# Up projections of a split-fp32 decoder trunk: six products of 288 columns a weight tile, against five of 384, 384, 384, 384 and 192

## What is computed

```python
h = rmsnorm(x, p["ffn_norm"][layer])
up = h @ p["w_up"][layer]                    # D_MODEL 1024 -> 2 * D_FF = 5632
c, fb = causal_dwconv(up, ffn_bufs[layer], p["ffn_conv_w"][layer], p["ffn_conv_b"][layer])   # 3 taps
x = x + (jax.nn.silu(c[..., :D_FF]) * c[..., D_FF:]) @ p["w_down"][layer]
```

## Time and profile before

| | |
|---|---|
| median of 3 runs | 1236.5 us (1236.37 to 1237.01) |
| the profiled execution's own time | 1235.46 us |
| its span | 1233.7 us |
| TensorE busy with matmuls | 1210.8 us (98%), 8828 matmuls |
| VectorE, ScalarE, GpSimd busy | 672.0, 455.9, 550.9 us (54%, 37%, 45%) |
| chain that ended last | 93% TensorE |

### The profile page before, as it was taken

One profiled execution on the slowest core, in us unless ns is written; L12 is line 12 of the kernel. 1 busy time (PEld: TensorE's weight loads), 2 busy tenths in 40 slices (PEclk: granted clock), 3 DMA queues, 4 the chain that ended last, 5 costly groups with the idle time before them and its releaser, 6 DMA issues.

```text
span 1233.7 us, 22991 instructions
## 1 busy us (share of the span) xinstructions
PE 1210.8 (98%) x8828; PEld 1180.7 (96%) x8828; DVE 672.0 (54%) x1080; ACT 455.9 (37%) x677; POOL 550.9 (45%) x524
## 2 busy tenths in 40 slices
PE   7999999999999999999999999999999999999996
PEld 7887899999999999999999999999999999999996
DVE  5999466786136741365513754377821676216742
ACT  7333364433123331234512533344321434214354
POOL 4643345565345443453455224346543454435430
PEclk9999999999999999999999999999999999999998
DMA  6310133222312223222422222222322222222222
GB/s 236 110 44 18 44 97 101 71 88 82 103 69 85 85 69 103 69 81 65 156 77 85 79 68 69 86 69 76 94 86 86 69 85 85 86 86 69 85 65 78
DMA packets 33636, 103.57 MB, mean 84 GB/s; under 512 B 4880, under 2 KB 6928, under 8 KB 33552
## 3 DMA queue, kind: packets, MB, share of 16 engines
q1 hardware_dynamic: 29344, 98.40, 24.5%
q10 hardware_dynamic: 4224, 4.22, 1.1%
HBM read 98.29 MB, written 4.79 MB: 84 GB/s over the span
## 4 chain that ended last, share of the span: by engine, by line
PE 93%; DVE 2%; ACT 2%; POOL 1%; issue 1%; DMA 0%; ACTq 0%; SPq 0%; DVEq 0%
PE psum L315 87%; PE psum L409 3%; DVE squares_sum L1466 1%; PE psum L353 1%; PE psum L560 1%; POOL w_lo L995 0%; DVE residual L1163 0%; PE psum L361 0%; ACT arena L917 0%; DVE arena L1435 0%; DMA w_raw<-in_w_in_ab 0%; PE psum L429 0%; DVE arena L1458 0%; ACT w_hi L625 0%; PE psum L423 0%
## 5 line engine op out<-in xcount | busy, mean ns | idle before, releaser
L995 POOL TENSOR_TENSOR w_lo<-w_raw,w_hi 128x1024 fp32r<-128x1024 f32 (+2 forms) x188 | 437.0, 2327 | 504.0 <-ACT w_hi L625 504.0
L315 PE MATMUL psum<-x_hi,w_hi 128*128 128x288 f32 x1856 | 401.7, 298 | 6.4 <-ACT w_hi L625 6.4
L315 PE MATMUL psum<-x_hi,w_lo 128*128 128x288 f32 x1856 | 398.0, 296 | 1.1 <-POOL w_lo L995 1.1
L315 PE MATMUL psum<-x_lo,w_hi 128*128 128x288 f32 x1856 | 397.8, 296 | 0.0
L315 PEld LDWEIGHTS psum<-x_hi,w_hi 128*128 128x128 f32 x1856 | 299.6, 189 | 8.6 <-ACT w_hi L625 6.4
L315 PEld LDWEIGHTS psum<-x_hi,w_lo 128*128 128x128 f32 x1856 | 299.6, 189 | 1.5 <-POOL w_lo L995 1.5
L315 PEld LDWEIGHTS psum<-x_lo,w_hi 128*128 128x128 f32 x1856 | 299.8, 189 | 0.0
L625 ACT ACTIVATE w_hi<-w_raw 128x1024 fp32r<-128x1024 f32 (+2 forms) x188 | 187.1, 997 | 237.7 <-PE psum L315 222.5
L1397 DVE SCALAR_TENSOR_TENSOR arena<-arena,params 128x592 f32<-128x592 f32 x176 | 205.7, 1169 | 84.7 <-ACT arena L841 71.3
L315 PE MATMUL psum<-h_hi,w_hi 128*128 128x288 f32 x960 | 207.3, 297 | 3.7 <-DVE residual L1163 1.9
L315 PE MATMUL psum<-h_hi,w_lo 128*128 128x288 f32 x960 | 205.6, 296 | 0.0
(11 more groups left out here) (140 smaller groups left out, 693.8 us busy)
## 6 DMA issues: line engine op xcount, KB each, us to landing
w_raw<-in_w_up SPq DMA_DIRECT2D x88, 512.0 KB, 3.2
w_raw<-in_w_down SPq DMA_DIRECT2D x32, 512.0 KB, 3.5
w_raw<-in_w_in_c SPq DMA_DIRECT2D x16, 512.0 KB, 3.2
w_raw<-in_w_in_ab SPq DMA_DIRECT2D x12, 512.0 KB, 3.6
w_raw<-in_w_down SPq DMA_DIRECT2D x16, 384.0 KB, 3.2
w_raw<-in_w_out_ab SPq DMA_DIRECT2D x16, 256.0 KB, 2.6
w_raw<-in_w_out_c SPq DMA_DIRECT2D x8, 512.0 KB, 3.2
residual<-in_x SPq DMA_DIRECT2D x8, 288.0 KB, 6.3
```

The costliest lines, as they stand in the source:

```text
L315: last = nc.tensor.matmul(PS[:, 2 * (q % 2 if slot is None else slot) + half, 0:HALF], w[q][:, k * P:(k + 1) * P], r[:, r_at, half * HALF: ...
L995: nc.gpsimd.tensor_tensor(w_lo[slot][:, 0:nk * P], w_raw[slot % 2][:, 0:nk * P], w_hi[slot][:, 0:nk * P].bitcast(F32), ALU.subtract).then_ ...
```

## The change

The operands `xh` and `xl` become two planes of one tile `xs`, so that one access pattern can take the same tokens of both. In the up-projection units alone (`wide=True`) the 576 tokens are divided into 384 (`FRONT`) and 192 (`BACK`). Per input tile there are five matmuls: hi·hi, hi·lo and lo·hi over the front, lo·hi over the back, and one of 384 columns that takes the back of `xh` and of `xl` side by side against `w_hi`, so that hi·hi and hi·lo of the back land beside each other in one bank. The sum of those two is made when the unit is read out: ScalarE copies the hi·lo part from the accumulator to `mixed[:, j]`, VectorE adds it to the hi·hi part in place, and then scales as before in pieces of 384, 128 and 64.

```diff
+    FRONT = 2 * T // 3
+    BACK = T - FRONT
...
-        xh = sb("x_hi", [P, KD, T], F32R)
-        xl = sb("x_lo", [P, KD, T], F32R)
+        xs = sb("x_split", [P, KD, 2, T], F32R)
+        xh, xl = xs[:, :, 0, :], xs[:, :, 1, :]
...
+        mixed = cut(F1 + 2 * T + RT * D, 2, BACK)
...
+            def wide_products(q, k, first, final):
+
+                slot, cols = q % 2, slice(k * P, (k + 1) * P)
+                front, both = PS[:, 2 * slot, 0:FRONT], PS[:, 2 * slot + 1, 0:2 * BACK]
+                nc.tensor.matmul(front, w_hi[q][:, cols], xs[:, k, 0, 0:FRONT], start=first, stop=False)
+                nc.tensor.matmul(front, w_hi[q][:, cols], xs[:, k, 1, 0:FRONT], start=False, stop=False)
+                nc.tensor.matmul(both.rearrange("p (a t) -> p a t", a=2), w_hi[q][:, cols], xs[:, k, :, FRONT:T],
+                                 start=first, stop=False)
+                nc.tensor.matmul(front, w_lo[q][:, cols], xs[:, k, 0, 0:FRONT], start=False, stop=final)
+                return nc.tensor.matmul(PS[:, 2 * slot + 1, 0:BACK], w_lo[q][:, cols], xs[:, k, 0, FRONT:T],
+                                        start=False, stop=final)
...
+                    if wide:
+                        last = wide_products(q, k, at == 0, at == nk - 1)
+                    else:
+                        last = products(q, k, r0 + k, nk, rh, rl, at == 0, at == nk - 1)
...
+                            act.wait_ge(unit_done, i * 2 + (u0 + j + 1))
+                            nc.scalar.activation(mixed[:, j, :], PS[:, 2 * j + 1, BACK:2 * BACK], ACT.Copy)\
+                                .then_inc(mix_ready, 1)
                             if j == 0 and before is not None:
                                 product_hi(before)
...
+            def scaled_mixed(slot, u, dst, pad, at):
+
+                bank = PS[:, 2 * slot + 1, 0:BACK]
+                dve.wait_ge(mix_ready, at)
+                nc.vector.tensor_tensor(bank, bank, mixed[:, slot, :], ALU.add).then_inc(mix_added, 1)
+                nc.vector.tensor_tensor(dst[:, pad:pad + FRONT], PS[:, 2 * slot, 0:FRONT], rstd[:, 0:FRONT], ALU.mult)
+                dve.wait_ge(mix_added, at)
+                nc.vector.tensor_tensor(dst[:, pad + FRONT:pad + PR], bank[:, 0:PR - FRONT], rstd[:, FRONT:PR], ALU.mult)
+                n = NS * (pad + DS)
+                nc.vector.tensor_tensor(smp(dst[:, pad + PR:pad + PR + n], pad + DS)[:, :, pad:],
+                                        smp(bank[:, PR - FRONT:BACK]), smp(rstd[:, PR:T]), ALU.mult)\
+                    .then_inc(acc_free, 1)
...
-                            scaled_padded(j, u, up[:, j, :], FB)
+                            scaled_mixed(j, u, up[:, j, :], FB, (i + c0) * 2 + (j + 1))
```

More of the change, by code:

```diff
@@ L226, in hybrid_trunk @@
         st_out = sem("st_out")
+        mix_ready, mix_added = sem("mix_ready"), sem("mix_added")
         tap0_ready, tap1_ready, tap_ready = sem("tap0_ready"), sem("tap1_ready"), sem("tap_ready")
@@ L323, in weights, with unit @@
                     pe.wait_ge(acc_free, u - 1)
-            def unit(q, u, nk, rh, rl, ready=None, base=0, middle=None, r0=0, order=None):
+            def unit(q, u, nk, rh, rl, ready=None, base=0, middle=None, r0=0, order=None, wide=False):
                 weights(u)
@@ L331, in unit @@
                         pe.wait_ge(ready, base + at + 1)
-                    last = products(q, k, r0 + k, nk, rh, rl, at == 0, at == nk - 1)
+                    if wide:
+                        last = wide_products(q, k, at == 0, at == nk - 1)
+                    else:
+                        last = products(q, k, r0 + k, nk, rh, rl, at == 0, at == nk - 1)
                     if middle is not None and at == nk // 2:
@@ L480, in _, with plain_units @@
                 yb_unit(m)
-            def plain_units(u0, nk, rh, rl, n):
+            def plain_units(u0, nk, rh, rl, n, wide=False):
                 with pe.Fori(0, n // 4) as i:
                     for q in range(4):
-                        unit(q, i * 4 + (u0 + q), nk, rh, rl)
+                        unit(q, i * 4 + (u0 + q), nk, rh, rl, wide=wide)
             def ffn(layer):
@@ L494, in ffn @@
                     if g == 0:
-                        unit(0, u0, KD, xh, xl, xl_ready, KD * n)
+                        unit(0, u0, KD, xh, xl, xl_ready, KD * n, wide=True)
                         norm_sums(n, r)
@@ L501, in middle @@
                             spread(r)
[L502 to L505, removed]
+                        unit(1, u0 + 1, KD, xh, xl, middle=middle, wide=True)
+                        unit(2, u0 + 2, KD, xh, xl, wide=True)
+                        unit(3, u0 + 3, KD, xh, xl, wide=True)
+                        plain_units(u0 + 4, KD, xh, xl, 2 * nt - 4, wide=True)
                     else:
-                        plain_units(u0, KD, xh, xl, 2 * nt)
+                        plain_units(u0, KD, xh, xl, 2 * nt, wide=True)
                     ud = u0 + 2 * nt
```

## The result

The changed kernel takes 1246.68 us (median of 4 runs, 1245.86 to 1247.48) against 1236.43 before: 10.3 us slower, ratio 1.0083, 95% interval 1.0065 to 1.0100. The forecast was 1245, slower. The time came out as predicted, but two terms of the sum were wrong, by some 17 and 15 us in opposite directions, and the rows show it at once.

What follows compares the result with a forecast made beforehand. TensorE was taken as the bound, with the VectorE, ScalarE and GpSimd loop second and expected to take over. -12.0 (products) + 21.6 (waits) - 1.1 = +8.5 on 1235.5, so 1244, stated as 1245; range 1227 to 1262.

Steps and rivals of the forecast that it cites:

- What bounds: TensorE bounds at 12.80 us a pair of up tiles; the VectorE, ScalarE and GpSimd loop, 12.57, is second.
- TensorE's part: Up-unit matmuls: 162.5 ns per 384 columns, a 133 ns floor for 192; input tile 783 ns, -12.0 us in all.
- The loop's length: VectorE, ScalarE and GpSimd in group 0: five links of read-out, copy, taps and `w_lo` lengthen a pair from 12.57 to 13.3 us.
- The loop's waits: TensorE waiting on late read-outs in the up groups: 10.8 us a layer, +21.6 for both, less 1.1 already there.
- the cost at the short down projection: After group 2's 6 pairs the last product comes late for a short down projection: 2.5 us.
- the tile (783 ns): Sign: one input tile of an up unit, four products at 162.5 ns plus one at 133, would take 783 ns.
- the 13.3 us in group 2: Sign: read-outs would come every 13.3 us in groups 1 and 2 as in group 0.
- the 20 us of waits: Sign: TensorE's waits would name VectorE's last scaling, some 20 us in all, against next to none before.
- the free tap and the blocked one: Sign: on VectorE the first tap after j = 1 runs free; the second is blocked by GpSimd's `w_lo`, ending 0.63 later.
- The slow narrow product: Rival, chance 0.12: the 192-column product takes 323 ns, a tile 973 ns, +122 us, 1358.
- A fee on the wide product and the floor on the narrow one: Rival, 0.08 shared with a slow side-by-side operand: products 173 and 133 ns, tile 825, +21, 1257.
- The side-by-side operand: Rival, 0.08 shared with fee and floor: operand of two 192-column runs slower than a plain one; time between 1257 and 1358.

Runs made afterwards that it cites:

- x2: Kernel before the change, products of 288 kept, but read out with the change's copy and add (values wrong): 1243.51 us, ratio 1.0057.
- y4: The change with tokens divided 320 and 256 instead of 384 and 192, ScalarE's order unchanged, whole computation: 1245.70 us, ratio 1.0077.
- y2: The change with tokens divided 320 and 256, without copy and add at read-out (part of the sum left out): 1232.25 us, ratio 0.9968.
- x1: The change's five products (384 and 192), without copy and add at read-out (part of the sum left out): 1241.45 us, ratio 1.0040.
- y1: Kernel before the change with three products of 512 and three of 64 columns per input tile in up units, plain read-out: 1395.19 us, one execution.
- x3: The change with ScalarE's copy put ahead of the rounding of the weight tile: 1243.46 us, ratio 1.0056.
- x4: The change with ScalarE's copy for j = 1 put ahead of the silu of j = 0: 1242.85 us, ratio 1.0052.
- z1: The change (384 and 192) with the early copy of x4 and both roundings of a pair moved to its start: 1245.43 us, ratio 1.0078.
- z2: As z1, with tokens divided 320 and 256, whole computation: 1242.42 us, ratio 1.0052.

## Why the prediction was right, and where it was wrong

- **What bounds**: right. The loop of VectorE, ScalarE and GpSimd in groups 0 was a second bound within 0.23 us a pair of the first, and the change pushed it over. x2 shows its part alone.
- **TensorE's part: the wrong step.** The forecast took the 13 ns at 288 columns for a floor from the weight load, "and not like a fee on every matmul", from the plain fp32 type's 2 ns over. The fee is there at every width of fp32r tried, 13 ns at 256, 288 and 320, 14 at 384, 18 at 512. The real floor is the load's own turn, 0.111 us. The earlier trace rows showed it: (1.21 - 0.19) / 9 = 0.113 us, where the forecast divided 1.21 by 10 and then took 133 all the same. The products that go with those ten loads, of the plain fp32 type, have one column each and stand within 1.17 us, so narrow products that cost less than 133 ns were there to be seen:

```profile
23.36 1.17 PE L353 MATMUL psum<-ones,squares_sum 128*128 128x1 f32 x10
```

  So 162.5 should have been 174, and 133 should have been 111: 807 ns instead of 783, +4.9 us instead of -12.0. The forecast weighed a floor (783) against a fee (786) and found them nearly the same; there are both, and the larger of the two counts at each width. The upper bound of the 384 product, 173, was the truth within 1 ns.
- **The loop's length**: right, link by link. Copy 0.32 (0.33 forecast), add 0.36 (0.35), from silu to tap 0 3.31 us against 1.55 before, which is the +1.76 forecast, 13.33 us a pair (13.3), the first tap free and the second blocked.
- **The loop's waits: too high, for two reasons.** 21.6 us less 1.1 were forecast, some 5 found. The first reason is the error above: against a pair of 12.91 instead of 12.53 us the excess is 0.42, not 0.8, and groups 1 and 2 then never use up their slack. The second is the step from the excess to the waits. y4, with a fast tile and an excess of 13.53 - 12.70 = 0.83 us, is the case that the forecast described. It is 13.5 us above y2, which has its products, and not 20.5. From first read-out to first read-out it took 5.5 and 5.6 us more than y2 in groups 0 (6.4 forecast), 1.4 in each group 1 (1.9), and from group 2 on 0.4 more and 0.4 less (2.5): the cost at the short down projection did not appear.
- **The total was right in part by luck.** TensorE's part was wrong by 17 us one way and the waits by 15 the other. About 8 of the 15 hang together with the first error, as a faster TensorE would have waited for the same loop; the other 7 are the overpriced waits, and only chance put them there. The right total is thus no evidence for its terms; the rows of the changed kernel, x1 and y4 decide. Of the signs named ahead, the tile (783 ns), the 13.3 us in group 2 and the 20 us of waits did not come; the 13.3 us in groups 0 and 1, the free tap and the blocked one did.
- **Rivals.** The slow narrow product did not occur. "A fee on the wide product and the floor on the narrow one" was the nearest, with the floor at 111 instead of 133 ns. The side-by-side operand is free within 1 ns at 384 columns.
- **The rule on the gap.** The Trainium skill's page "TensorE: Matmul & The Clock Gate", section "Back-to-back issue gap", gives N / 2.4 + 2.5 ns. The row of 288 columns spoke against that, and y1 and y2 bear it out for this type: 231 ns at 512 columns, where the rule would give 216. The hint that came with it, that a change at equal columns brings next to nothing, was nearer to the outcome than the -12 us.

## What to carry to other kernels

Take a fee per matmul from the same type and at two widths before pricing a new division; merging products saves their fee only if no piece falls below the turn of a weight load. When an engine pair runs within a few per cent of the bound, a read-out instruction handed to another engine costs what stands ahead of it in that engine's order, not its own 0.3 us. Look there first, and try it further ahead: x3 and x4 took 0.29 and 0.49 us back of the 0.76 that a pair had grown by. Then ask what the moved work releases on the other engines, which z1 and z2 had not. A conversion of excess into waits is a term like any other and wants a run of its own. And check two terms of opposite sign one by one, as they can cancel.

## What the runs showed of the hardware

The turn of an fp32r product with 128x128 weights, at the 2.4 GHz level, was 120 ns at 256 columns, 133 at 288, 147 at 320, 174 at 384, 231 at 512. Products of 64 and 192 columns add 111 ns to a tile, the turn of a weight load, part of it on the place of the next product. The plain fp32 type had 242 ns a pass for 288 columns, 2 ns over two cycles a column. Why the one type pays 13 to 18 ns and the other 2 stays open; no run was made on it. VectorE's instructions with both inputs in SBUF wait out a whole `w_lo` of GpSimd's if they start inside it (up to 3.0 us instead of 0.83), and those that read an accumulator do not (the adds and scalings kept 0.36 and 0.55 us beside it), so moving work by 0.2 us can turn a blocked instruction into a free one.
